# A mixture-of-experts pass on one core: the first bias leaves TensorE for GpSimd and VectorE, the clamps move to GpSimd, and the scatter skips empty places

## The reference

```python
hcat = x_pad[tok] @ w1[e] + b1[e]                        # 1024 -> 2048
x_glu = jnp.minimum(hcat[:, ::2], 7.0)                   # even columns
x_lin = jnp.clip(hcat[:, 1::2], -7.0, 7.0)               # odd columns
act = x_glu * jax.nn.sigmoid(1.702 * x_glu) * (x_lin + 1.0)
y = act @ w2[e] + b2[e]                                  # 1024 -> 1024
out = sum over a token's 4 experts of weight * y
```

## Time and profile before

| | |
|---|---|
| median of 3 runs | 3124.48 us (3121.29 to 3132.78) |
| profiled execution, its own time | 3126.25 us |
| its span, first to last instruction | 3124.4 us |
| TensorE, matmuls | busy 2940.8 us, 94% |
| VectorE | busy 2114.5 us, 68% |
| ScalarE | busy 1587.8 us, 51% |
| GpSimd | busy 279.4 us, 9% |
| TensorE's mean granted clock | 0.964 of full speed |

### The profile page before, as it was taken

The page is one execution under the profiler, slowest core; times in us unless marked ns, Lnnn a source line. Parts: engine busy times, 40 slices in busy tenths (PEclk is TensorE's granted clock), DMA queues, the critical chain, the costliest instruction groups (busy, mean ns, idle before and its releaser), DMA issues. The chain is left out here.

```text
span 3124.4 us, 46233 instructions
## 1 busy us (share of the span) xinstructions
PE 2940.8 (94%) x18534; PEld 2353.0 (75%) x18534; DVE 2114.5 (68%) x2176; ACT 1587.8 (51%) x1767; POOL 279.4 (9%) x225
## 2 busy tenths in 40 slices
PE   5999999789999999999999959898899999899999
PEld 4777787468778788887877847788778877678877
DVE  6567654569989899999999975566463454456642
ACT  3556433347777777777777734222454542333321
POOL 0110010001111111111111000343000000000000
PEclk9999999789999999999999979899999998999999
DMA  6322343369999999999999972000221222323321
GB/s 247 126 92 85 108 152 108 112 249 368 369 370 367 370 375 378 374 369 371 371 365 373 365 259 68 16 4 4 92 66 58 75 70 69 120 73 95 95 88 68
DMA packets 217372, 607.95 MB, mean 195 GB/s; under 512 B 10784, under 2 KB 118304, under 8 KB 183424
## 3 DMA queue, kind: packets, MB, share of 16 engines
q1 hardware_dynamic: 202480, 554.87, 48.2%
q0 software_dynamic: 14592, 50.36, 4.7%
q10 hardware_dynamic: 144, 0.53, 0.1%
HBM read 582.62 MB, written 23.10 MB: 194 GB/s over the span
## 5 line engine op out<-in xcount | busy, mean ns | idle before, releaser
L2481 DVE TENSOR_TENSOR weight_ring_part<-weight_ring,weight_ring_part 128x2048 fp32r<-128x2048 f32 x380 | 852.8, 2286 | 107.6 <-ACT weight_ring_part L2420 107.1
L2420 ACT ACTIVATE weight_ring_part<-weight_ring 128x2048 fp32r<-128x2048 f32 x380 | 714.3, 1915 | 258.8 <-PE ps L193 135.2
L193 PE MATMUL ps<-weight_ring_part 128*128 128x512 f32 x1456 | 580.0, 398 | 0.0
L293 DVE TENSOR_TENSOR weight_ring_part<-weight_ring,weight_ring_part 128x2048 fp32r<-128x2048 f32 x111 | 253.2, 2281 | 237.4 <-ACT weight_ring_part L290 234.9
L189 PE MATMUL ps<-weight_ring_part,gathered_hi 128*128 128x512 f32 x1024 | 408.9, 399 | 0.0
L193 PE MATMUL ps<-weight_ring_part,gathered_hi 128*128 128x512 f32 x1024 | 405.3, 396 | 0.0
L192 PE MATMUL ps<-weight_ring_part,gathered_lo 128*128 128x512 f32 x1024 | 405.3, 396 | 0.0
L189 PE MATMUL ps<-h1T_hi,weight_ring_part 128*128 128x512 f32 x872 | 359.7, 412 | 3.1 <-DVE weight_ring_part L293 1.7
L192 PE MATMUL ps<-h1T_hi,weight_ring_part 128*128 128x512 f32 x872 | 348.4, 400 | 0.0
L193 PEld LDWEIGHTS ps<-weight_ring_part 128*128 128x128 f32 x1456 | 277.4, 191 | 69.9
L290 ACT ACTIVATE weight_ring_part<-weight_ring 128x2048 fp32r<-128x2048 f32 x111 | 211.0, 1901 | 132.2 <-PE ps L193 104.0
(11 more groups left out here) (491 smaller groups left out, 4386.4 us busy)
## 6 DMA issues: line engine op xcount, KB each, us to landing
weight_ring<-in_w SPq DMA_DIRECT2D x190, 2048.0 KB, 9.0
weight_ring<-in_w_in SPq DMA_DIRECT2D x58, 1024.0 KB, 5.2
weight_ring<-in_w_ffn_up SPq DMA_DIRECT2D x44, 512.0 KB, 5.0
weight_ring<-in_w_ffn_down SPq DMA_DIRECT2D x11, 1024.0 KB, 4.8
mod_tile<-in_w_ada POOLq DMA_DIRECT2D x36, 256.0 KB, 3.1
weight_ring<-in_w_ada SPq DMA_DIRECT2D x8, 1024.0 KB, 12.9
gate_rows<-in_w_ada POOLq DMA_DIRECT2D x28, 256.0 KB, 3.2
weight_ring<-in_w_branch SPq DMA_DIRECT2D x6, 1024.0 KB, 5.6
```

Of the source, the lines that this page charges most:

```text
L193: return nc.tensor.matmul(out, x[0], y[1], start=False, stop=stop)
L293: self.nc.vector.tensor_tensor(lo, full, hi, ALU.subtract).then_inc(self.split, 1)
L2420: nc.scalar.activation(hi_half(h), full_half(h), ACT.Copy).then_inc(w_rounded, 1)
L2481: nc.vector.tensor_tensor(lo_half(h), full_half(h), hi_half(h), ALU.subtract).then_inc(w_split, 1)
```

## The change

Three edits. **The first bias:** the four bias matmuls, the rounding of the bias on ScalarE, its low part on VectorE and the two small set-up copies on ScalarE go. SyncE loads the bias as two rows of 1024 values into one partition; GpSimd copies each row to all 128 partitions (`spread_bias`, two `partition_broadcast` of 1024 values per expert); VectorE adds it while it reads the banks. **The clamps:** VectorE's two tensor_scalar (clamp) per half become two tensor_tensor (add) from PSUM and the bias, and GpSimd clamps glu and lin in SBUF (`clamp`, four tensor_scalar of 128x512 per expert). ScalarE's activation waits for the clamped glu, VectorE's product for the clamped lin. **The scatter** gets a bound of 2047, so that places with a row above it are skipped. In GpSimd's order, clamp(e+1) and spread_bias(e+2) stand between gather(e+3) and scatter(e).

```diff
-                    sp.dma_start(b1_full[:, :], row.rearrange("e (n f) -> (e n) f", n=4)).then_inc(b1_loaded, 16)
+                    for n in range(2):
+                        sp.dma_start(b1_rows[n], row[:, DFF * n:DFF * n + DFF]).then_inc(b1_loaded, 16)
...
-                        sp.wait_ge(used, t.half(0)[0] + (1 + free0))
+                        sp.wait_ge(b1_ready, t.i + 1)
                         load_b1(t.e + 1)
...
+                def spread_bias(r, e):
+                    pool.wait_ge(b1_loaded, 32 * (r * E + e) + 32)
+                    for n in range(2):
+                        last = nc.gpsimd.partition_broadcast(b1_wide[:, DFF * n:DFF * n + DFF], b1_rows[n], channels=P)
+                    last.then_inc(b1_ready, 1)
+
+                def clamp(r, e):
+                    for s in range(2):
+                        half = slice(512 * s, 512 * s + 512)
+                        pool.wait_ge(glu_ready, (r * E + e) * 2 + (s + 1))
+                        nc.gpsimd.tensor_scalar(glu[:, half], glu[:, half], LIMIT, None, ALU.min).then_inc(glu_clamped, 1)
+                        pool.wait_ge(lin_ready, (r * E + e) * 2 + (s + 1))
+                        nc.gpsimd.tensor_scalar(lin[:, half], lin[:, half], -LIMIT, LIMIT, ALU.max, ALU.min).then_inc(lin_clamped, 1)
+
                 def scatter(r, e):
                     pool.wait_ge(y_read, r * E + e + 2)
-                    nc.gpsimd.indirect_dma_start(y_rows, bass.IndirectOffsetOnAxis(y_at[:, e:e + 1], 0), y_out[:, e % 2, :], None)\
+                    nc.gpsimd.indirect_dma_start(y_rows, bass.IndirectOffsetOnAxis(y_at[:, e:e + 1], 0), y_out[:, e % 2, :], None,
+                                                 bounds_check=TOPK * T - 1, oob_is_err=False)\
                         .then_inc(y_stored[e % 2], 16)
...
+                    spread_bias(r, 0)
+                    clamp(r, 0)
+                    spread_bias(r, 1)
...
+                        if e + 1 < E:
+                            clamp(r, e + 1)
+                        if e + 2 < E:
+                            spread_bias(r, e + 2)
                         scatter(r, e)
...
-                    pe.wait_ge(b1_ready, t.i + 1)
                     pe.wait_ge(up_read, t.i + 1)
-                    for n in range(4):
-                        nc.tensor.matmul(ps[:, n, :], b1_pick[:, n:n + 1].to_broadcast([36, P]), b1_parts[:, :], start=True, stop=False)
...
-                        if t.more:
-                            round_b1(t.i + 1)
                         for s in range(2):
-                            act.wait_ge(glu_ready, t.i * 2 + (s + 1))
+                            act.wait_ge(glu_clamped, t.i * 2 + (s + 1))
...
-                        if t.more:
-                            split_b1(t.i + 1)
-
+                        dve.wait_ge(b1_ready, t.i + 1)
                         dve.wait_ge(used, t.half(7)[0] + (1 + free0))
                         for s in range(2):
                             pairs = ps[:, 2 * s:2 * s + 2, :].rearrange("p b (n two) -> p b n two", two=2)
                             half = slice(512 * s, 512 * s + 512)
-                            nc.vector.tensor_scalar(glu[:, half].rearrange("p (b n) -> p b n", b=2), pairs[:, :, :, 0], LIMIT, None,
-                                                    ALU.min).then_inc(glu_ready, 1)
-                            last = nc.vector.tensor_scalar(lin[:, half].rearrange("p (b n) -> p b n", b=2), pairs[:, :, :, 1], -LIMIT, LIMIT,
-                                                           ALU.max, ALU.min)
-                        last.then_inc(up_read, 1)
+                            bias = b1_wide[:, 1024 * s:1024 * s + 1024].rearrange("p (b n two) -> p b n two", b=2, two=2)
+                            nc.vector.tensor_tensor(glu[:, half].rearrange("p (b n) -> p b n", b=2), pairs[:, :, :, 0], bias[:, :, :, 0], ALU.add)\
+                                .then_inc(glu_ready, 1)
+                            nc.vector.tensor_tensor(lin[:, half].rearrange("p (b n) -> p b n", b=2), pairs[:, :, :, 1], bias[:, :, :, 1], ALU.add)\
+                                .then_inc(lin_ready, 1)
+                        nc.vector.engine_nop().then_inc(up_read, 1)
...
                             half = slice(512 * s, 512 * s + 512)
+                            dve.wait_ge(lin_clamped, t.i * 2 + (s + 1))
                             dve.wait_ge(act_ready, t.i * 2 + (s + 1))
                             nc.vector.scalar_tensor_tensor(lin[:, half], lin[:, half], 1.0, glu[:, half], ALU.add, ALU.mult)\
```

More of the change, by code:

```diff
@@ L2152, in build @@
         xg_lo = sb(experts, "gathered_lo", [P, DK, P], F32R)
-        b1_pick = sb(experts, "b1_pick", [36, 4], F32R)
-        b1_full = sb(experts, "b1_full", [4, 512])
-        b1_parts = sb(experts, "b1_parts", [36, 512], F32R)
+        b1_late = sb(experts, "b1_late", [1, DFF])
+        b1_rows = (gate_rows[0:1, 0, :], b1_late[:, :])
+        b1_wide = sb(experts, "b1_wide", [P, 2 * DFF])
         glu = sb(experts, "glu", [P, DFF])
@@ L2242, in experts_pass @@
             (hot_ready, table_ready, table_read, x_turned, xg_rounded, xg_ready, up_read,
-             glu_ready, act_ready, hidden_ready, turned, hid_rounded, hid_ready, y_read, y_free,
-             b1_loaded, b1_rounded, b1_ready, w_rounded, w_split, b2_summed, b2_added, used, *loaded) = sems
+             glu_ready, lin_ready, glu_clamped, lin_clamped, act_ready, hidden_ready, turned, hid_rounded, hid_ready, y_read, y_free,
+             b1_loaded, b1_ready, w_rounded, w_split, b2_summed, b2_added, used, *loaded) = sems
             b2_banks = lambda t: ps[:, (0, 2, 6, 6)[t]:(0, 2, 6, 6)[t] + 2, :]
@@ L2345, in up @@
                             f = slice(512 * n, 512 * n + 512)
-                            last = product(nc, ps[:, n, :], (x_hi, x_lo), (w_hi[:, f], w_lo[:, f]), False, k == DK - 1)
+                            last = product(nc, ps[:, n, :], (x_hi, x_lo), (w_hi[:, f], w_lo[:, f]), k == 0, k == DK - 1)
                         last.then_inc(used, 1)
@@ L2420, in round_half @@
                     nc.scalar.activation(hi_half(h), full_half(h), ACT.Copy).then_inc(w_rounded, 1)
-                def round_b1(n):
-                    act.wait_ge(b1_loaded, n * 16 + 16)
-                    nc.scalar.activation(b1_parts[0:4, :], b1_full[:, :], ACT.Copy).then_inc(b1_rounded, 1)
                 def round_inputs(n):
@@ L2438, in prologue @@
                 def prologue(t):
-                    round_b1(t.i)
                     if rounds:
@@ L2470, in on_scalar @@
                 with when_needed(act):
-                    nc.scalar.activation(b1_pick[:, :], K["b1_pick"][0:36, 0:4], ACT.Copy)
-                    nc.scalar.activation(b1_parts[:, :], const[0:36, 0:512], ACT.Copy, scale=0.0)
-                    act.drain()
                     act.nop().then_inc(y_read, 1)
@@ L2481, in split_half @@
                     nc.vector.tensor_tensor(lo_half(h), full_half(h), hi_half(h), ALU.subtract).then_inc(w_split, 1)
-                def split_b1(n):
-                    dve.wait_ge(b1_rounded, n + 1)
-                    nc.vector.tensor_tensor(b1_parts[32:36, :], b1_full[:, :], b1_parts[0:4, :], ALU.subtract).then_inc(b1_ready, 1)
                 def split_inputs(n):
@@ L2513, in prologue @@
                         dve.drain().then_inc(up_read, 1)
-                    split_b1(t.i)
                     if rounds:
@@ L2572, in build @@
         pass_sems = ["hot_ready", "table_ready", "table_read", "x_turned", "xg_rounded", "xg_ready", "up_read",
-                     "glu_ready", "act_ready", "hidden_ready", "turned", "hid_rounded", "hid_ready", "y_read", "y_free",
-                     "b1_loaded", "b1_rounded", "b1_ready", "w_rounded", "w_split", "b2_summed", "b2_added", "halves_used"]
+                     "glu_ready", "lin_ready", "glu_clamped", "lin_clamped", "act_ready", "hidden_ready", "turned", "hid_rounded", "hid_ready", "y_read", "y_free",
+                     "b1_loaded", "b1_ready", "w_rounded", "w_split", "b2_summed", "b2_added", "halves_used"]
         first_tiles = ring.units[block2_at:block2_at + 2]
```

## The result

The changed kernel takes 3310.06 us (median of 4 runs, 3305.92 to 3314.72) where the kernel before takes 3124.48 (3121.29 to 3132.78 over 4 runs): a ratio of 1.058, 95% interval 1.056 to 1.060. It is 186 us slower; 3114 was predicted, with 3160 as the upper end. Lines are those of the changed kernel: adds 2546 and 2548, clamps 2305 (glu) and 2307 (lin), copies 2298, scatter 2311, gather 2292, load of the bias 2253, activation 2475, product 2559, tokens' split 2497, half splits 2492, TensorE's transposes of the hidden values 2428. In the kernels of the experiments the same lines stand a few numbers further down.

What follows compares the result with a forecast made beforehand. TensorE's own sequence was taken to set the 36.55 us turn. Removing 1.11 us of bias matmuls, less VectorE-GpSimd collisions, left 0.3 per turn: 9 us, plus 2 in the first turn, giving 3114 us; range 3100 to 3128, widened to 3160.

Steps and rivals of the forecast that it cites:

- 1.4 was taken: GpSimd's copy of 1024 values to all partitions: 1.4 us assumed, between 1.05 (two memsets) and 2.08 (two tensor_tensors).
- the rival in which they do not: Copies do not stop VectorE, clamps alone cost 0.9 us: the whole 36 us gained, 3088 us; chance 0.22.
- the walk's upper end of 37.0: Turn with all collisions summed: half 12 split 1.6 us late for TensorE, 0.5 more than the gain; 36.55 + 0.5.
- TensorE waits for half 12: Sign of collisions: half 12 split at 1226.3, wanted by TensorE at 1224.71, so 1.6 us late.
- I take 0.65, nearer to the memset: GpSimd's clamp of 128x512: 0.65 us assumed, between the memset's 0.526 and the two-input tensor_tensor's 1.040.
- the prediction's own walk through the turn: One expert turn in time order from the adds at 1214.42: clamps to 1217.10, tokens split 1223.87, half 12 at 1226.3.
- far from its bound: GpSimd's load per turn: 5.4 us of clamps and copies beside 3.5 already there, so not limiting.
- VectorE becomes the bound: Rival: VectorE loses over 3.5 us per turn; with copies of 2.08, 38.1 per turn, 3168 us; chance 0.29.
- its worst case: VectorE as the bound with clamps of 1.04, three standing in its way: 39.5 us per turn, 3210 us.
- I put nothing in for it: GpSimd loading code: zero counted, from an 8 ns trace entry; about 6 us for a first call would give 3120.
- The 36 us of TensorE's matmuls: Bias matmuls off TensorE: 1.11 us per turn, 34.4 for 31 turns, plus 2.0 in the first; 36.4 together.
- the third rival: Transfers hold the turn: if the skip saves no time, turn near 36.4, 3115 to 3120 us; chance 0.07.

Runs made afterwards that it cites:

- e1: Changed kernel without its four GpSimd clamps per expert (output not clamped), bias copies kept: 3140.89 us, 1.0039 of the kernel before.
- m3: e2 with a small GpSimd clamp of 128x8 between glu's first clamp and lin's, no code change: 3276.02 us, 1.0472 of the kernel before.
- k2: e2 with a GpSimd copy of 8 numbers per expert where the wide copies were: 3293.99 us, 1.0531 of the kernel before.
- f1: Changed kernel with 18 useless matmuls on TensorE in its stall ahead of the transposes: 3306.6 us, 1.056 of the kernel before.
- f2: Changed kernel with one VectorE drain ahead of half 11, so that lin's clamp can start first: 3287.39 us, 1.0493 of the kernel before.
- m1: k2 with one VectorE drain ahead of the split of half 11: 3226.04 us, 1.0311 of the kernel before.
- e2: Changed kernel with its clamps, but bias copied only for the first expert and used for all: 3197.79 us, 1.0208 of the kernel before.
- e3: Changed kernel with neither clamps nor copies after the first expert: 3109.87 us, 0.9939 of the kernel before.
- h2: Changed kernel with GpSimd's wait for the last scatter moved behind the clamps, and f2's drain: 3251.85 us, 1.0386 of the kernel before.

## Why the prediction was wrong

**Right.** The four bias matmuls are gone from TensorE, adds in place of clamps cost nothing, the skip gains nothing by itself, the scatter is not late by its own work, a copy takes 1.30 us alone (1.4 was taken), and VectorE and GpSimd stop each other. The copies met VectorE, so the rival in which they do not falls; beside the splits the first copy takes 2.85 us in the median, over the 2 us that the prediction named as a sign of being wrong. e1, 3141 with a turn of 36.86, is what such collisions cost: below the walk's upper end of 37.0, and TensorE waits for half 12 as it said.

**The term that was mis-sized: the clamp.** "I take 0.65, nearer to the memset." Alone it takes 1.54 (glu, one operation) and 1.93 (lin, two), above even the two-input product of 1.04 that was to be the upper bound; an operation with one input and two scalars is not bounded by a row with two inputs. With the measured prices the prediction's own walk through the turn comes out right: glu from +0.79 to +2.33; half 11 at +2.41 goes just before lin's clamp, where the walk had three clamps done by then; lin's ends at +6.48; glu at +8.57, lin at +10.57, product, tokens' split at +12.49. The walk had +9.45 (1223.87 - 1214.42).

**The step that failed: "far from its bound".** GpSimd's load was added up as busy time per turn, 5.4 and 3.5 us, and what the clamps do to others was looked for in one place, the split of half 12. TensorE's wait before that, for the tokens' split, was not asked for: TensorE wants it at 1223.74, and the walk itself had it at 1223.87, with nothing to spare. No engine's busy sum got near the turn. What counts is latency: VectorE's in-order list waits for four clamps in a row ahead of the tokens' split, TensorE waits 4.29 us for that, and then runs at the lower clock, which costs 2.5 us more in the turn shown. None of the rivals had this; "VectorE becomes the bound" had the sign, and even its worst case, 3210 with clamps of 1.04, had VectorE fuller, where it emptied from 89.7 to 77.1.

**Left out: code changes.** "I put nothing in for it", on an entry of 8 ns in the earlier trace rows. That stage had one; a turn now has two, of 8.3 and 12.4 us. The Trainium skill (GPSIMD Engine Reference, "Instruction dispatch") has about 6 us for a first call; here it is more, and comes again at each alternation between copy and clamp. The changes cost by two ways: 0.04 us more in the clamp behind them, which let half 11 go first (m3 alone, 78 us of k2's 96), and a round of GpSimd of 42 us, which makes clamps late as soon as the path is shorter (f1, f2). In m1, 28 us above e2, the 5 turns with a late clamp take 42.3 us and the others 39.5, where e2 has 39.0: half of the 28 is lateness, the rest is not explained.

**The gain.** The 36 us of TensorE's matmuls were 21 in e3 (turn 36.03 instead of 35.4). The waits read as the third rival had it, TensorE with 1.11 us less to do meets the transfers: it idles 0.5 us in a turn for splits, where it idled 0.1. No run tests this apart.

From e3's 3110: clamps in the better order 88 (e2), code changes with the worse order 96 (k2), wide instead of small copies 16: 3310. Each step is the difference of two kernels that ran, and holds in this order only: with lin's clamp first in nearly all turns, wide instead of small copies are h2 against m1, 26 us. Why a clamp is 0.04 us slower behind a change, and why the second change is 4 us longer than the first, was not settled.

## What to carry to other kernels

Before work is handed from one in-order engine to another and back, walk the round trip in order of time with the receiver's single durations, and not by its busy share: an engine that is idle for two thirds can hold all the others. Where two engines shut each other out, see which instruction comes first and by how much: a lead of 0.04 us decided over 2 us of each turn here. And keep one kind of GpSimd work in a loop, or leave it a whole idle stretch for each change.

## What was not expected of the hardware

- On GpSimd a change from clamps to copies takes 8.3 us in the turn shown (5.5 to 9.4 over the changed kernel's run), one from the scatter and gather to clamps 12.4, behind entries of 11 ns.
- A clamp of 128x512 on GpSimd takes 1.50 to 1.54 us with one operation and 1.93 with two, more than a product of two inputs (1.04). VectorE does one of 128x1024 in 0.69 to 0.70.
- GpSimd's instruction behind VectorE's split waits for all of it (4.08 instead of 1.93), VectorE's split behind GpSimd's clamp lost 0.43. And a clamp on VectorE, with one input in SBUF, took 1.8 instead of 0.70 beside a copy.
- TensorE that idled 4.29 us did its transposes in 1.97 us (to the end of the last; 1.03 before) and the matmuls behind them at 0.43 instead of 0.235, at a granted clock of 0.50. After 1.27 us of idling, in one turn of e2, the transposes took 1.09 at a granted clock of 1.00. In the changed kernel they also took 1.09 in 5 turns with 3.3 to 3.9 us of idling; there the lower clock came behind them (3.15 us for seven intervals).
